# Order of an expert's weights and of its context sums in the first mixture-of-experts layer of a one-core transformer kernel

## The reference, cut to what matters

```python
def expert_choice_ffn(h, router_w, w_gate, w_up, w_down):
    B, n, D = h.shape
    cap = EC_CAPACITY * n // N_EXPERTS          # 64 rows of 512 latents, 32 rows of 256 context rows
    aff = jax.nn.softmax((h @ router_w).astype(F32), axis=-1)
    gate, idx = lax.top_k(jnp.swapaxes(aff, 1, 2), cap)
    xe = jax.vmap(lambda hb, ib: hb[ib])(h, idx)
    a = jnp.einsum('becd,edf->becf', xe, w_gate)
    u = jnp.einsum('becd,edf->becf', xe, w_up)
    ye = jnp.einsum('becf,efd->becd', jax.nn.silu(a) * u, w_down) * gate[..., None].astype(h.dtype)
    return jax.vmap(lambda ib, yb: jnp.zeros((n, D), h.dtype).at[ib.reshape(-1)].add(yb.reshape(-1, D)))(idx, ye)
```

## Time and profile before

| what | value |
|---|---|
| median of 3 runs | 3700.16 us (3699.72 to 3703.6) |
| the profiled execution: its time / its span | 3697.88 us / 3695.9 us |
| PE busy over the span | 92% |
| DVE, ACT busy | 32%, 18% |
| the chain that ended last, PE's share | 84% |
| 16 DMA engines, mean | 159 GB/s |
| granted TensorE clock, mean | 0.960 of 2.4 GHz |
| the experts of the first layer | from 2087.9 to 2797.4 us, 709.5 us |

### The profile page before, as it was taken

The page is one execution under the profiler, slowest core; times in us unless marked ns, Lnnn a source line. Parts: engine busy times, 40 slices in busy tenths (PEclk is TensorE's granted clock), DMA queues, the critical chain, the costliest instruction groups (busy, mean ns, idle before and its releaser), DMA issues.

```text
span 3695.9 us, 34379 instructions
## 1 busy us (share of the span) xinstructions
PE 3396.2 (92%) x14238; PEld 1554.5 (42%) x14238; DVE 1198.9 (32%) x2281; ACT 649.4 (18%) x1425; POOL 0.2 (0%) x4
## 2 busy tenths in 40 slices
PE   7999888999988899898967799999998999699998
PEld 3444443444444344454845433333333554333332
DVE  1111552111183334763564312222223472311112
ACT  1000441000052211110112111111102161211111
POOL 0000000000000000000000000000000000000000
PEclk9999999999999899999978899999999999899999
DMA  3333202233300112101311277767783100599996
GB/s 149 137 137 141 87 1 78 91 137 137 142 41 35 70 71 97 49 23 52 139 55 47 92 300 280 277 261 276 276 311 138 52 1 24 214 420 420 420 419 267
DMA packets 86380, 588.01 MB, mean 159 GB/s; under 512 B 12296, under 2 KB 13227, under 8 KB 15828
## 3 DMA queue, kind: packets, MB, share of 16 engines
q1 hardware_dynamic: 78624, 572.56, 39.2%
q10 hardware_dynamic: 7604, 13.27, 1.1%
HBM read 583.69 MB, written 2.10 MB: 158 GB/s over the span
## 4 chain that ended last, share of the span: by engine, by line
PE 84%; DVE 10%; ACT 4%; issue 1%; DMA 1%; ACTq 0%; another core or an unknown queue 0%; DVEq 0%; PEldq 0%
PE ps L466 14%; PE ps L1713 12%; PE ps L1061 7%; PE ps L807 5%; PE ps L463 4%; PE ps L1328 4%; PE ps L1643 4%; PE ps L1625 3%; PE ps L1737 3%; PE ps L1725 3%; PE ps L1757 3%; PE ps L1973 2%; PE ps L1152 2%; DVE mem L771 1%; PE ps L490 1%; PE ps L1206 1%
## 5 line engine op out<-in xcount | busy, mean ns | idle before, releaser
L466 PE MATMUL ps<-mem 128*128 128x512 f32 x1152 | 505.1, 597 | 1.9 <-DVE mem L584 1.9
L1713 PE MATMUL ps<-mem 128*64 128x512 f32 x2048 | 467.4, 599 | 1.3 <-ACT mem L1661 0.7
L466 PEld LDWEIGHTS ps<-mem 128*128 128x128 f32 x1152 | 218.6, 191 | 284.0 <-issue 281.7
L1713 PEld LDWEIGHTS ps<-mem 128*64 128x64 f32 x2048 | 137.1, 137 | 291.1 <-issue 287.6
L1061 PE MATMUL ps<-mem 128*128 128x512 f32 (+1 forms) x768 | 253.1, 492 | 0.3 <-ACT mem L913 0.3
L1683 DVE SCALAR_TENSOR_TENSOR mem<-ps,mem 128x512 f32<-128x512 f32 x128 | 96.1, 751 | 359.4 <-PE ps L1643 356.3
L1061 PEld LDWEIGHTS ps<-mem 128*128 128x128 f32 x768 | 147.3, 193 | 107.1 <-issue 96.3
L807 PE MATMUL ps<-mem 128*128 128x512 f32 x384 | 175.2, 612 | 13.3 <-DVE mem L887 11.5
L463 PE MATMUL ps<-mem 128*128 128x512 f32 x384 | 167.0, 594 | 0.0
L527 ACT ACTIVATE mem<-ps 128x512 f32<-128x512 f32 x48 | 28.7, 598 | 683.2 <-PE ps L466 683.2
L1328 PE MATMUL ps<-mem 128*128 128x512 f32 (+1 forms) x384 | 143.4, 535 | 5.5 <-DVEq L164 5.5
(11 more groups left out here) (287 smaller groups left out, 3806.7 us busy)
## 6 DMA issues: line engine op xcount, KB each, us to landing
mem<-in_moe_w SPq DMA_DIRECT2D x384, 1024.0 KB, 7.9
mem<-in_w_in SPq DMA_DIRECT2D x48, 1024.0 KB, 9.0
mem<-in_ada_w SPq DMA_DIRECT2D x48, 1024.0 KB, 6.8
mem<-in_hy_w_in SPq DMA_DIRECT2D x24, 1024.0 KB, 6.9
mem<-in_w_out SPq DMA_DIRECT2D x12, 1024.0 KB, 9.0
mem<-in_k_win_l SPq DMA_DIRECT2D x8, 1024.0 KB, 6.8
mem<-in_hy_w_out SPq DMA_DIRECT2D x8, 1024.0 KB, 6.1
mem<-in_sw_w_in SPq DMA_DIRECT2D x6, 1024.0 KB, 5.9
```

The lines of the kernel that those rows point to most:

```text
L466: m = mm(ps[:, j % 4, :], Wc[s][:, k, t * P:(t + 1) * P], HTL[:, k, :], start=(k == 0), stop=(k == KD - 1))
L1713: m = mm(ps[64 * x:64 * x + 64, pair, :], lat(k), w[x][:, k % 4, :], start=(k == 0), stop=(k == KD - 1))
```

## The change

In the first layer the twelve half slots of an expert are stored and consumed as three groups of four: gate and up of all hidden columns for the first half of the features, the same for the second half, and the four of the down matrix (`expert_slots`, `halves_first`). A new function, `pe_moe_both`, runs the first layer. In a feature half it does the latent products of both pairs and then the context products of both, which lie in four column groups by (pair, gate or up), so that each context sum is complete in its group. The product with `PAIR` is gone; the context of an expert is copied out, transposed, passed through silu and multiplied by up once (`pe_turn_ctx`, `silu_ctx`, `product_ctx`) instead of twice. A group of four is waited for at its start, and its second matmul gives back the four of the group before. The ring of the first layer has eight half slots: the six of before and two at the end of the arena, open one phase before the layer.

The core of the diff (the same four-at-a-time use holds for the down group):

```diff
@@ PLACE, the ring
-        PLACE = [n % WSLOTS for n in range(BEFORE_LAST)] + [LAST_RING[m % len(LAST_RING)] for m in range(12 * N_EXP)]
+        BEFORE_FIRST = DEPTH * N_HYB + sum(HY_SLOTS)
+        FIRST_RING = [(BEFORE_FIRST + i) % WSLOTS for i in range(WSLOTS)] + [WSLOTS + 5, WSLOTS + 6]
+        FIRST_OPEN = PHASES_TO_SWA - 4
+        PLACE = [n % WSLOTS for n in range(BEFORE_FIRST)]
+        PLACE += [FIRST_RING[m % len(FIRST_RING)] for m in range(12 * N_EXP)]
+        BEFORE_LAST = len(PLACE) + 6 + 4
+        PLACE += [FIRST_RING[m % WSLOTS] for m in range(6 + 4)]
+        LAST_RING = [FIRST_RING[(10 + i) % WSLOTS] for i in range(WSLOTS)] + list(range(WSLOTS, WSLOTS + XSLOTS))
+        PLACE += [LAST_RING[m % len(LAST_RING)] for m in range(12 * N_EXP)]
@@ the new order on PE
+        def pe_moe_both(A, m_, st):
...
+                for kh in range(2):
+                    ks = range(4 * kh, 4 * kh + 4)
+                    w = [Wh[st.get_half(x)] for x in range(4)]
+                    for pair in range(2):
+                        if kh == 0 and e:
+                            A.e.wait_ge(S["act_out"], 2 * (e - 1) + pair + 1)
+                        for k in ks:
+                            for x in range(2):
+                                m = mm(ps[64 * x:64 * x + 64, pair, :], lat(k), w[2 * pair + x][:, k % 4, :],
+                                       start=(k == 0), stop=(k == KD - 1))
+                                if k == 4 * kh and pair == 0 and x == 1 and (e or kh):
+                                    m.then_inc(S["w_used"], 4)
+                        if kh:
+                            m.then_inc(A.mark("psum_full"), 1)
+                        if kh and pair == 0:
+                            pe_aux(A, m_, (e, 1, 1))
+                    if kh:
+                        pe_turn(A, m_, e, 0)
+                        pe_aux(A, m_, (e, 2, 1))
+                    else:
+                        pe_aux(A, m_, (e, 0, 0))
+                        if e:
+                            A.e.wait_ge(S["ctx_out"], e)
+                    for k in ks:
+                        for pair in range(2):
+                            for x in range(2):
+                                r = 64 * pair + 32 * x
+                                m = mm(ps[r:r + CAP_C, 4, :], cxt(k), w[2 * pair + x][:, k % 4, :], start=(k == 0), stop=(k == KD - 1))
...
+                pe_turn(A, m_, e, 1)
+                pe_aux(A, m_, (e, 3, 1))
+                w = [Wh[st.get_half(x)] for x in range(4)]
...
+                    if k == 3:
+                        pe_turn_ctx(A, m_, e)
+                m.then_inc(A.mark("o_full"), 1)
+                pe_aux(A, m_, (e, 4, 1))
+                A.e.wait_ge(S["ctx_hidden"], e + 1)
...
+                m.then_inc(A.mark("ctx_o_full"), 1)
+                if e == N_EXP - 1:
+                    st.done(A, 4)
+                else:
+                    st.next(4)
+                pe_aux(A, m_, (e, 5, 0))
+                pe_aux(A, m_, (e, 5, 1))
@@ the turn
-            if m_.ctx:
-                A.e.wait_ge(S["ctx_out"], 2 * e + pair + 1)
-                if e or pair:
-                    A.e.wait_ge(S["ctx_hidden"], 2 * e + pair)
-                for k in range(4):
-                    m = mm(ps[:, 6, k * 2 * CAP_C:(k + 1) * 2 * CAP_C], m_.GUC[:, k * P:(k + 1) * P], m_.PAIR,
-                           start=True, stop=True)
-                m.then_inc(A.mark("ctx_turned"), 1)
+        def pe_turn_ctx(A, m_, e):
+
+            A.e.wait_ge(S["ctx_out"], e + 1)
+            if e:
+                A.e.wait_ge(S["ctx_hidden"], e)
+            for k in range(4):
+                m = tr(ps[:, 6, k * P:(k + 1) * P], m_.GUC[:, k * P:(k + 1) * P], IDENT)
+            m.then_inc(A.mark("ctx_turned"), 1)
@@ the weights' layout on the host
-            out[:, 4 * at + 2 * half], out[:, 4 * at + 2 * half + 1] = x[cx, half], y[cy, half]
+            to = 4 * half + 2 * at if halves_first and at < 2 else 4 * at + 2 * half
+            out[:, to], out[:, to + 1] = x[cx, half], y[cy, half]
```

More of the change, by code:

```diff
@@ L1453, in act_load_gate @@
             e.dma_start(m_.IO, a["k_iota"]).then_inc(S["const_in"], 16)
-            if m_.ctx:
-                e.dma_start(m_.PAIR, a["k_pair"]).then_inc(S["const_in"], 16)
-            e.wait_ge(S["const_in"], 48 if m_.ctx else 32)
+            e.wait_ge(S["const_in"], 32)
         def act_moe_a(A, m_):
@@ L1718, in pe_moe_d @@
                         pe_aux(A, m_, (e, 2 * pair + kh, 0))
[L1719 to L1726, removed]
                         st.next()
@@ L1777, in pe_moe_d @@
             end_phase(A)
+        def pe_moe_both(A, m_, st):
+            pe_aux(A, m_, "first")
+            for e in range(N_EXP):
+                XS = m_.XS[e // GROUP % 2]
+                lat = lambda k: XS[:, k, e % GROUP, 0:CAP_L]
+                cxt = lambda k: XS[:, k, e % GROUP, CAP_L:]
+                if e % GROUP == 0:
+                    A.e.wait_ge(*m_.evacuated(gathered(m_, e // GROUP)))
+                for kh in range(2):
[26 more added lines that the diff above has]
+                                m = mm(ps[r:r + CAP_C, 4, :], cxt(k), w[2 * pair + x][:, k % 4, :], start=(k == 0), stop=(k == KD - 1))
+                    if kh:
+                        m.then_inc(A.mark("ctx_full"), 1)
+                    else:
+                        pe_aux(A, m_, (e, 0, 1))
+                    st.next(4)
[3 more added lines that the diff above has]
+                if e:
+                    A.e.wait_ge(S["e_ready"], e)
+                for k in range(KD):
+                    if k % 4 == 0:
+                        A.e.wait_ge(S["c_ready"], 2 * e + k // 4 + 1)
+                    for x in range(2):
+                        m = mm(ps[64 * x:64 * x + 64, 7, :], m_.AT[:, k, :], w[k // 4 * 2 + x][:, k % 4, :],
+                               start=(k == 0), stop=(k == KD - 1))
+                        if k == 0 and x == 1:
+                            m.then_inc(S["w_used"], 4)
+                    if k == 3:
[3 more added lines that the diff above has]
+                A.e.wait_ge(S["ctx_hidden"], e + 1)
+                if e:
+                    A.e.wait_ge(S["ctx_o_out"], e)
+                for k in range(KD):
+                    for x in range(2):
+                        r = 64 * x + 32 * (k % 2)
+                        m = mm(ps[r:r + CAP_C, 5, :], m_.ATC[:, k, :], w[k // 4 * 2 + x][:, k % 4, :],
+                               start=(k < 2), stop=(k >= KD - 2))
+                m.then_inc(A.mark("ctx_o_full"), 1)
+                if e == N_EXP - 1:
+                    st.done(A, 4)
+                else:
+                    st.next(4)
+                pe_aux(A, m_, (e, 5, 0))
+                pe_aux(A, m_, (e, 5, 1))
+            pe_aux(A, m_, "last")
+            end_phase(A)
@@ L1811, in silu, with silu_ctx @@
                     A.e.wait_ge(S["o_full"], e)
-                act(m_.AT[:, 4 * pair:4 * pair + 4, :], turned_parts(2, CAP_L)[0], ACT.Silu)\
+                act(m_.AT[:, 4 * pair:4 * pair + 4, :], turned_parts()[0], ACT.Silu)\
                     .then_inc(A.mark("b_ready"), 1)
[L1814 to L1819, removed]
+            def silu_ctx(e):
+                A.e.wait_ge(S["ctx_turned"], e + 1)
+                if e:
+                    A.e.wait_ge(S["ctx_o_full"], e)
+                act(ctx_hidden(m_), turned_ctx_parts()[0], ACT.Silu).then_inc(A.mark("ctx_silu"), 1)
             act_aux(A, m_, "first")
@@ L1847, in dve_moe_d, with copy @@
         def dve_moe_d(A, m_):
[L1848 to L1851, removed]
+            def copy(e):
+                A.e.wait_ge(S["ctx_full"], e + 1)
+                if e:
+                    A.e.wait_ge(S["ctx_turned"], e)
                 nc.vector.tensor_copy(m_.GUC, ps[:, 4, :]).then_inc(A.mark("ctx_out"), 1)
@@ L1883, in dve_moe_d @@
                 if m_.ctx:
-                    copy(e, 1)
-                dve_aux(A, m_, (e, 3, 1))
-                product(e, 1)
+                    copy(e)
+                    product(e, 1)
+                    dve_aux(A, m_, (e, 3, 1))
+                    product_ctx(e)
+                else:
+                    dve_aux(A, m_, (e, 3, 1))
+                    product(e, 1)
                 dve_aux(A, m_, (e, 4, 1))
```

71 lines of the change are left out of this document (28 added, 43 removed).

## The result

| | before | changed |
|---|---|---|
| median of 7 runs | 3700.91 us | 3712.33 us |
| range | 3698.65 to 3707.9 | 3706.37 to 3720.37 |
| profiled execution: time / span | 3697.88 / 3695.9 | 3711.56 / 3709.8 |

The ratio is 1.0029, with a 95% interval of [1.0017, 1.0042]: slower by some 11 us. The measured 3712 lies inside the forecast's range, 10 us above its value of 3702, and the chance stood on the wrong side: I gave 0.52 to no measurable change and 0.25 to slower.

What follows compares the result with a forecast made beforehand. The prediction took PE's instructions, one after the other, to bound the first layer's experts. Its terms, -31 + 19.3 + 9 + 3 + 2.5 = +2.8 us, taken as +2, gave 3702 us, range 3689 to 3714.

Steps and rivals of the forecast that it cites:

- PE's work: First layer's experts: no products with `PAIR`, one more turn, longer runs; 1.94 us less per expert, 31 us over 16.
- The ring: First layer's weight loads: a group of four cannot be shorter than 13.4 us, making PE wait 19.3 us with undisturbed transfers.
- Late landings: Weight loads landing late: 0.55 us per group of four on average, 9 us in all, from 4 to 14.
- Waits for weights: PE's waits in the first layer's experts: 19.3 us with undisturbed transfers and 9 us for late landings.
- Jobs in bank 3: Side jobs behind the context's down products: yc and gc wait 0.8 us for ACT's copy of job g; together 3 us.
- The clock: Experts 12 to 15: PE's waits of 2.8 us and more bring two clock drops, 2.5 us, from none to 6.
- Rival 2: Waits for weights pull PE's clock down: four to six drops, late landings 14 us, +12 us, 3712, slower; chance 0.20.
- The sum: Whole kernel: -31 + 19.3 + 9 + 3 + 2.5 = +2.8 us, taken as +2; median 3702 us.
- Rival 3: First layer's groups of four load below 420 GB/s from empty queues: 14.3 us per group, about +17 us, 3717; chance 0.07.

Runs made afterwards that it cites:

- experiment 1: The changed kernel, but PE waits for a group's third and fourth half slot only where it first needs them; 3670.0 us, ratio 0.9918.
- half loads: The changed kernel with only half the columns of each half slot loaded in the first expert layer, from the ninth load on; 3668.6 us, ratio 0.9915.
- early give-back: The changed kernel, still waiting for four at once, with gate-and-up groups given back at their own end; 3689.7 us, ratio 0.9973.
- experiment 7: Experiment 1's kernel plus a PE wait in each expert behind the context's down products until DVE copied them out; 3739.9 us, ratio 1.0110.
- experiment 3: Same run as half loads: the changed kernel with half the bytes per half slot in the first expert layer; 3668.6 us, ratio 0.9915.
- experiment 5: Same run as early give-back: the changed kernel with gate-and-up groups given back at their own end; 3689.7 us, ratio 0.9973.
- experiment 6: Experiment 1's kernel plus a PE wait in each expert behind the latents' down products until ACT copied them out; 3689.4 us, ratio 0.9970.
- experiment 8: Experiment 1's kernel with the fourth job y behind the context's turn, job g behind the latents' down products, gc ahead of yc; 3656.9 us, ratio 0.9885.

## Why the prediction was right and wrong, by its steps

- **PE's work, -31 us: right.** With no wait for weights and as many slow stretches as before (experiment 1) the stage is 30.9 us shorter, with 0.8 us more of other waits: -31.7. Some of the agreement is luck: the sum takes the context's turn at 0.49 us, while the prediction's own list of the down group has it at 0.59, as it was then measured; that is 1.6 us over 16 experts.
- **The ring, 13.4 us at least for a group: right.** 13.52 in the rows above. The quickest of the 46 groups of four landed 12.1 us after its first issue and the middle one 12.3, for 12.2 forecast. The half loads, the early give-back and the waits in twos each act on another part of this sum, and each took away the waits that hang on it.
- **Late landings, 0.55 us on average: right**, 0.6 (mean 12.8). Waits for weights: 28.3 us forecast (19.3 and 9), 31.0 measured.
- **Jobs in bank 3, +3 us: too high.** ACT's waits rose by 4.8 us, but DVE's fell by 4.0; together +0.8. At experts 7, 11 and 15 I had counted the moved job g as worth nothing; its own work and its wait lie inside the stall for DVE, which shrinks by as much.
- **The clock, "two drops, 2.5 us, from none to 6": wrong, and the step that put the chance on the wrong side.** There are seven more slow stretches than before. The changed kernel's stage is 43.7 us longer than that of experiment 1, of which 31.0 are waits for weights; in the rest PE is busy 698.1 us instead of 685.5 for the same 3784 records. Of these 12.6 us, the 23.9 us more at half the clock can make up to 11.9; the last 0.7 or so is not shown to be the clock. I had let only waits of 2.8 us and more count, from one pair of rows, and 1.25 us each. In fact seven of the nine waits of 2.0 us and more had a slow stretch behind them, those of 2.1 to 2.3 us among them, and one costs up to 1.7 us. The other two of the nine slow stretches stand behind no long wait at all, but behind two short ones close together, for job g's copy and for DVE. This is the first of the two, at the end of expert 7, where the granted clock from 2451.0 to 2454.3 us is 0.50:

```profile
2447.78 1.13 PE L1653 MATMUL ps<-mem 128*128 128x256 f32 x4 [0.69 <-ACT mem L1675]
2450.47 0.44 PE L1644 MATMUL ps<-mem 128*128 128x128 f32 x2 [1.55 <-DVE mem L1693]
2450.84 8.79 PE L1775 MATMUL ps<-mem 128*64 128x512 f32 x32
```

- **What was luck.** Rival 2 had the mechanism and, at 3712, the very number, but the number is in part luck: it had the late landings at 14 us (31.0 - 19.3 = 11.7 measured), the jobs at 3 (0.8), the clock at 7 (12.6), and its waits were to be longer than 2.5 us. That 3712 lies in the stated range is owed to this rival having been taken into it; the clock's own bounds, none to 6 us, did not hold.
- **The sum.** -31.7 (PE) + 31.0 (weights) + 0.8 (jobs) + 12.6 (clock, nearly all of it) = +12.7 us, for a measured growth of the stage of 12.8.
- **Rival 3 falls.** From empty queues the second, third and fourth half slot mostly land 2.5 us apart, as at 420 GB/s. The Trainium skill's rule (DMA: Bandwidth & Descriptors, "Where 436 GB/s comes from") that the HBM side binds at about 358 GB/s is not borne out by any run of this case; an estimate by its figure, 4.7 us for the first half slot and 2.93 for each further one, gives 13.5 us for the quickest group, and it needed 12.1. (The terms of this rival add up to about +16 us, not +17; nothing hangs on it.)

What stays open is why some waits of equal length have a slow stretch behind them and others have not: in experiment 7 thirteen of sixteen like waits had one. The counts are of one execution each; the mean granted clock of the kernel before alone went from 0.955 (3711.2 us) to 0.964 (3689.6 us) over 19 executions.

## What to carry to other kernels

When loads are grouped more coarsely, ask two things of the ring apart from its size: how much work lies between the give-back that lets a transfer start and the first use of what it brings, and whether the wait for a group stands at its start or at the first use of each part. Here a wait moved to the first use, 3.5 to 4.6 us later, was worth 42 us, and made a loss of 0.3% a gain of 0.8%. And while a transfer sets the length of a group, do not judge other savings in it: the side jobs moved gave nothing before that was mended and, with gc and yc exchanged as well, 13 us after.

## What the runs showed of the hardware that I had not expected

Idle time of PE has a second price. Sixteen idle stretches of 1.3 us among full work had no effect on the granted clock; of sixteen of 3.0 us thirteen were followed, 2.3 to 5.3 us after PE stopped, by a stretch at 1.2 GHz, and the clock's cost was 28.5 us on 46.6 us of idle time. Two shorter waits with one job between them can do it too. Such pairs, 0.69 us and then 1.55 or 1.18, stand at experts 7, 11 and 15 in the changed kernel and in experiments 1, 3, 5 and 6, and in each of these profiles two of the three had a slow stretch behind them; in experiment 8, where gc stands ahead of yc, the pairs are gone and so is every slow stretch. SP's four issues of a group mostly start 0.4 to 0.5 us apart, but in 6 of the 46 groups of the changed kernel two neighbours lie 1.1 to 1.7 us apart. All six are among the 17 groups whose last half slot landed more than 13 us after the first issue, and some of them also have a late first landing (6.8 us instead of 4.8), as in this one of the changed kernel, issued from 2387.8 us on:

```profile
L284 SPq DMA_DIRECT2D mem<-in_moe_w x4: 328/758/1496, 2387.8 to 2390.9; - x4
...
DMA to landing us min/median/max: 6.8/9.4/11.2
```
